# Four unused tensors in the SBUF layout of a transformer layer's kernel

## The reference

```python
u = x * (1.0 + sc1) + sh1
x = layer_norm(ALPHA * x + 0.5 * (1.0 + g1) * swiglu(u, ffn1_wg[l], ffn1_wu[l], ffn1_wd[l]), ln_g[l, 0], ln_b[l, 0])
u = x * (1.0 + sc2) + sh2
h = u @ w_in[l]
...
y = jnp.concatenate([o_nsa, o_mla], axis=-1) @ w_out[l]
x = layer_norm(ALPHA * x + (1.0 + g2) * y, ln_g[l, 1], ln_b[l, 1])
u = x * (1.0 + sc3) + sh3
x = layer_norm(ALPHA * x + 0.5 * (1.0 + g3) * swiglu(u, ffn2_wg[l], ffn2_wu[l], ffn2_wd[l]), ln_g[l, 2], ln_b[l, 2])
```

## The kernel before

| stage | stationary | moving | before | with the change |
|---|---|---|---|---|
| `ffn1A` | left, `ffn1A_*_hi/lo` | right, `ffn1S_*` | 160 and 0 | 0 and 0 |
| `ffn1B` | left, `ffn1B_h_*` | left, `ffn1B_wd_*` | 160 and 160 | 0 and 0 |
| `in` | right, `mix_in_u_*` | left, `in_w_*` | 0 and 128 | 0 and 0 |
| sparse, scores | left, `nsa_q` | left, `sparse_k_*` | 192 and 128 | 0 and 0 |
| sparse, apply | left, `sparse_v` | left, `nsaa_turned_*` | 128 and 192 | 0 and 0 |
| latent inputs | left, `queries_q_*`, `latent_kv_*` | left, `latent_in_uq_*`, `latent_ukv_*` | 128 and 128 | 0 and 0 |
| latent, scores and apply | left, `mla_q_*`, `latent_v` | left, `mla_k_*`, `mlaa_turned_*` | 128 and 128 | 0 and 0 |
| `out` | right, `mix_out_u_*` | left, `out_w_*` | 0 and 128 | 0 and 0 |
| `ffn2A` | left, `ffn2A_*_hi/lo` | right, `ffn2S_*` | 0 and 0 | 0 and 0 |
| `ffn2B` | left, `ffn2B_h_*` | left, `ffn2B_wd_*` | 0 and 0 | 0 and 0 |

## Time and profile before

### The profile page before, as it was taken

The page is one execution under the profiler, slowest core; times in us unless marked ns, Lnnn a source line. Parts: engine busy times, 40 slices in busy tenths (PEclk is TensorE's granted clock), DMA queues, the critical chain, the costliest instruction groups (busy, mean ns, idle before and its releaser), DMA issues. The chain is left out here.

```text
span 2456.2 us, 29088 instructions
## 1 busy us (share of the span) xinstructions
PE 2212.3 (90%) x10593; PEld 1824.4 (74%) x10593; DVE 1514.7 (62%) x2164; ACT 963.8 (39%) x1874; POOL 815.6 (33%) x665
## 2 busy tenths in 40 slices
PE   3899999979998899799998899896899999969993
PEld 3677888868887688688887788784688888857783
DVE  6866777636556614487887577635754445457667
ACT  4222323322234221777876466515333333312222
POOL 4355556534442000132211000003344444334443
PEclk9899999989998899899998899898899999989997
DMA  6244554344442310300000000312122222254442
GB/s 243 82 146 155 168 170 155 120 163 142 153 138 74 127 47 29 110 1 1 1 1 1 1 1 1 114 33 103 60 78 78 88 93 77 86 193 133 142 144 109
DMA packets 167875, 230.84 MB, mean 94 GB/s; under 512 B 15473, under 2 KB 113841, under 8 KB 167736
## 3 DMA queue, kind: packets, MB, share of 16 engines
q1 hardware_dynamic: 159672, 199.65, 24.8%
q0 software_dynamic: 8064, 29.36, 3.5%
HBM read 193.32 MB, written 35.66 MB: 93 GB/s over the span
## 5 line engine op out<-in xcount | busy, mean ns | idle before, releaser
L623 POOL TENSOR_TENSOR ffn_raw_u<-ffn_raw_u,ffn_gate 128x1024 f32<-128x1024 f32 x44 | 115.5, 2625 | 150.4 <-DMA ffn_raw_u<-in_ffn_wd 150.2
L663 PE MATMUL ffn_banks<-ffn2B_wd_hi,ffn2B_h_hi 128*128 128x512 f32 x352 | 140.1, 398 | 21.1 <-DVE ffn2B_h_lo L643 20.9
L623 POOL TENSOR_TENSOR ffn_raw_g<-ffn_raw_g,ffn_gate 128x1024 f32<-128x1024 f32 x44 | 109.6, 2490 | 138.3 <-DMA ffn_raw_g<-in_ffn_wd 132.4
L663 PE MATMUL ffn_banks<-ffn1B_wd_hi,ffn1B_h_hi 128*128 128x512 f32 x352 | 138.2, 393 | 13.4 <-DVE ffn1B_h_lo L643 13.4
L663 PE MATMUL ffn_banks<-ffn2B_wd_hi,ffn2B_h_lo 128*128 128x512 f32 x352 | 137.9, 392 | 0.0
L663 PE MATMUL ffn_banks<-ffn2B_wd_lo,ffn2B_h_hi 128*128 128x512 f32 x352 | 137.9, 392 | 0.0
L663 PE MATMUL ffn_banks<-ffn1B_wd_lo,ffn1B_h_hi 128*128 128x512 f32 x352 | 137.5, 391 | 0.0
L663 PE MATMUL ffn_banks<-ffn1B_wd_hi,ffn1B_h_lo 128*128 128x512 f32 x352 | 137.5, 391 | 0.0
L575 DVE TENSOR_TENSOR ffn2A_u<-ffn2A_u,ffn_banks 128x512 f32<-128x512 f32 x66 | 45.4, 687 | 144.5 <-PE ffn_banks L544 136.4
L544 PE MATMUL ffn_banks<-ffn1S_s_hi,ffn1A_t_hi 128*128 128x512 f32 x264 | 106.4, 403 | 12.8 <-DVE ffn1S_s_lo L490 12.8
L544 PE MATMUL ffn_banks<-ffn2S_s_hi,ffn2A_t_hi 128*128 128x512 f32 x264 | 103.8, 393 | 12.8 <-DVE ffn2S_s_lo L490 12.8
(11 more groups left out here) (383 smaller groups left out, 6699.4 us busy)
## 6 DMA issues: line engine op xcount, KB each, us to landing
ada_rows<-in_w_ada POOLq DMA_DIRECT2D x56, 512.0 KB, 4.7
ffn_raw_g<-in_ffn_wg SPq DMA_DIRECT2D x44, 512.0 KB, 3.9
ffn_raw_u<-in_ffn_wu SPq DMA_DIRECT2D x44, 512.0 KB, 5.2
ffn_raw_g<-in_ffn_wd SPq DMA_DIRECT2D x44, 512.0 KB, 3.5
ffn_h_raw<-hidden SPq DMA_DIRECT2D x88, 256.0 KB, 3.6
ffn_raw_u<-in_ffn_wd SPq DMA_DIRECT2D x44, 512.0 KB, 3.6
early_w<-in_w_ada SPq DMA_DIRECT2D x16, 512.0 KB, 7.6
early_x<-in_x SPq DMA_DIRECT2D x4, 2048.0 KB, 13.7
```

Of the source, the lines that this page charges most:

```text
L623: pool.tensor_tensor(self.wd(n), self.wd(n), self.gate[:, :], ALU.mult).then_inc(self.gated, 1)
L663: last = pe.matmul(self.banks[:, at, :], h[m][:, i * P:(i + 1) * P], w[m][:, e * HALF:(e + 1) * HALF], start=(f == 0 and p == 0), stop=(f ...
```

## The change

Four tensors are allocated and never used: 128 bytes per partition ahead of `all_ident` at the very start of the left side, 224 bytes in the first FFN behind `ffn1_c_col`, 192 bytes behind `sparse_rstd` ahead of the sparse stages, and 128 bytes in the second FFN behind its `ffn2_offset`. Everything allocated after one of them on the left, within its scope, moves up by its size. No instruction is added, taken away or moved. The right side stays where it is.

```diff
@@ feed_forward_first @@
     norm_rows, c_col = s.sb("norm_rows", [8 * DC, P]), s.sb("c_col", [P, DC])
+    s.sb("base", [P, 56])
     ffn = SplitFfn(nc, s, "ffn1", *weights, h_dram, ident)
@@ feed_forward_last @@
     gain, offset = s.sb("gain", [P, DC]), s.sb("offset", [P, DC])
+    s.sb("base", [P, 32])
     ffn = SplitFfn(nc, s, "ffn2", *weights, h_dram, ident)
@@ layer @@
     with Scope(nc, "all") as a, Scope(nc, "far", side="right") as far:
+        a.sb("base", [P, 32])
         ident = a.sb("ident", [P, P])
@@ layer @@
                 rstd = b.sb("rstd", [P, 2, TT])
+                b.sb("base", [P, 48])
                 sparse_inputs(nc, "sparse_in", h, table, gates, ident, (cmp_k_pos, cmp_v_pos), (cmp_k_w1, cmp_v_w1),
```

## The result

| | before | with the change |
|---|---|---|
| median | 2457.24 us (6 runs, 2454.80 to 2461.55) | 2443.58 us (6 runs, 2442.26 to 2447.62) |
| ratio of times, changed to before, and its 95% interval | | 0.9946 (0.9934 to 0.9959) |
| span of the profiled execution | 2456.2 us | 2440.5 us |
| mean granted clock | 0.956 | 0.955 |

The change makes the kernel 13.7 us faster by the medians; the two profiled executions differ by 15.7 us.

What follows compares the result with a forecast made beforehand. The prediction took the kernel to be bound by how often PE can start a matmul in stretches without waits. Savings of 7.9 + 1.5 + 5.6 + 2.2 + 0.5 = 17.7 us took 2457.9 to 2440 us, range 2433 to 2451 (8 in 10).

Steps and rivals of the forecast that it cites:

- The reading of the cause: Gapless matmul streams: 13.4 ns above the columns when both operands' remainders modulo 256 agree, 19 to 20 ns otherwise.
- Step 1: First FFN's product phase, ffn1A: spacing falls from 233.4 to 226.7 ns; 7.9 us steady plus 1.5 us early.
- The steady part: Last 14 of ffn1A's 22 steps, 1176 matmuls saving 6.7 ns each: 7.9 us.
- The early part: First 8 steps of ffn1A, where PE waits for DVE: 1.5 us taken, 4.5 at most, below nothing possible.
- Step 2: Input projection `in`, 768 matmuls of 494 columns saving 7.3 ns each: 5.6 us, bounds 0 and 5.6.
- Rival A: Odd width: `in` keeps 226.5 ns because 494 columns fall out of step with weight loads; 2446, chance 0.13.
- Step 3: Output projection `out`, 384 matmuls saving 5.6 ns each, from 232.3 to 226.7: 2.2 us.
- Step 4: Sparse attention, operands brought to equal remainders: 2 ns for 440 wide matmuls, 0.9 us at most, 0.5 taken.
- Step 5: ffn1B, ffn2A, ffn2B and the latent inputs keep equal remainders: 0 us.
- rival B: Gain given back in the down projection: ffn1B falls into ffn2B's slower rhythm, 8.0 us; 2448, chance 0.11.
- Rival C: Remainders aren't the cause; something else slows ffn1A and the projections, and stays; 2458, chance 0.08.
- Rivals D and E: First: operands at equal places modulo 2048 collide, 2463, chance 0.05. Second: pads misplace an operand; no sum changes, no chance given.

Runs made afterwards that it cites:

- k1_both_160: Changed kernel with both operands of ffn1A at 160, only the stationary one of ffn2A at 160, weights of both projections at 64; 2457.27 us.
- k3_128_64_192: Changed kernel with the stationary operand at 128 in ffn1A and 64 in ffn2A, the moving one at 192 in `in` and `out`; 2464.93 us.
- k4_small_shifts: Changed kernel with the stationary operand at 224 in ffn1A and 32 in ffn2A, the moving one at 32 in `in`, 160 in `out`; 2469.62 us.
- k7_changed_again: The changed kernel measured a second time, nothing altered; median 2441.13 us, ratio to before 0.9927.
- k2_moving_160: Changed kernel with ffn2A's moving operand at 160, ffn1A's stationary at 192, both operands of `in` at 128, `out`'s weights at 32; 2464.65 us.
- k12_whose_weights: Changed kernel with only u_lo of `out` at 128 and the four weight buffers of `in` at 96, 112, 128 and 160; 2444.17 us.
- k11: Changed kernel with the four weight buffers of `in` at 176, 184, 192 and 224; 2440.84 us.
- k6: Changed kernel with both projections put back to their layout before the change, weights at 128; median 2443.72 us, ratio to before 0.9943.
- k10: Changed kernel with the weights of `in` at 192; median 2437.72 us, ratio to before 0.9928.

## Why the prediction was right, and where it wasn't

The forecast was 2440 with a range of 2433 to 2451; the median is 2443.6. The sum was 17.7 us, of which 13.7 came by the medians and 15.7 by the two profiled executions. The stages that the sum names gave 13.5 us (9.4 + 2.4 + 1.6 + 0.1); that the profiled total is nearer to the forecast is luck, by the 2.1 us between stages, which the sum doesn't have.

*The reading of the cause* (equal remainders) holds for all streams of 512 columns. The decisive evidence ahead of the change was `ffn1B`, fast at 160 and 160; `k1_both_160` made the same in `ffn1A`, and made `ffn2A` slow by 160 and 0.

*Step 1, `ffn1A`.* The steady part is exact: a step of 84 matmuls went from 19.60 to 19.04 us, 14 of them 7.8 us (forecast 7.9), and neither DVE nor POOL became the limit. The early part was forecast at 1.5 and came at 1.6, but that agreement is luck. The early windows shown above have PE busy 58.9 of 60 us and 73.4 of 80, the latter at a mean clock of 0.96 where it was 1.00 before. Part of this is a stretch of 3.4 us at the lower level, in these windows of before and of the changed kernel:

```profile
169.00:177.00 8.00, 5.34 (x23) 4.37 (x24) 7.50 (x8) 4.18 (x8) 6.82 (x7) 1.00 0.25 69
169.00:177.00 8.00, 5.89 (x20) 4.56 (x19) 7.23 (x8) 4.44 (x8) 6.83 (x7) 0.79 0.27 84
```

It is there, near 170 us, in all eleven traces with `ffn1A` at 226.7 or 228.9 ns and in none of the three at 233.3; what brings it isn't shown. At half the clock it can take back up to 1.7 us of PE's time. The prediction named a falling clock as a risk and gave it no price of its own. PE's and DVE's waits there in the changed kernel, to set beside the earlier trace rows (waited for: us in total, times, longest us):

```profile
PE ffn_banks L544 <- DVE ffn1A_u L575: 7.6, 5, 3.3
```

```profile
DVE ffn1A_c L575 <- DMA hidden<-ffn1A_c: 25.2, 6, 5.3
DVE late_part_late L864 <- DMA ada_rows<-in_w_ada: 13.0, 7, 3.2
...
DVE ffn1A_c L575 <- PE ffn_banks L544: 3.0, 3, 1.6
```

The last of them was, before:

```profile
DVE ffn1A_c L575 <- PE ffn_banks L544: 9.5, 4, 3.7
```

As argued, the faster PE arrives sooner at the same chain: DVE's wait for the stores of the hidden tile grew from 18.4 to 25.2 us, its wait for PE fell from 9.5 to 3.0, and their sum stayed at 28 us; PE's own wait for L575 went from 8.6 to 7.6, so the sign that the prediction named for a failure of this step, a growing wait, didn't come. How much of the 4.5 us gets through differs from one execution to the next. Over the nine traces with `ffn1A` at 0 and 0 the stage took 456.6 to 462.0 us, with the changed kernel's 462.0 the longest and a middle value of 459.1. Against the one trace of before (471.4) that is 9.4 to 14.8. So the early part gave between 1.6 and 7.0, beyond the upper bound of 4.5, which priced only the matmuls' own spacing. But before's 471.4 looks like a long one: the two other traces with `ffn1A` at 233.3 ns, `k3_128_64_192` and `k4_small_shifts`, have 468.9 and 469.1. Against their 469.0 the early part gave -0.8 to 4.6, about what the prediction allowed.

*Step 2, `in`.* This is the term that was mis-sized: 5.6 us forecast, 2.4 measured (1.4 in `k7_changed_again`, where PE also waited 8.1 us for the first weights in place of 7.2). The spacing fell to 223.4, not to 219.2, so the sign that the prediction set for itself, 219 to 220 ns, failed. The step took the excess of the 512- and 384-column streams, 13.4 ns, over to 494 columns; at equal remainders it is 17.5 for 494 (and 16.6 for 480). Rival A was half right: the width does put `in` out of step, but the start matters all the same, only with its best place elsewhere (192). No row of before had a 494-column stream at another remainder, and the range said so; the value taken lay at the far end of 0 to 5.6 where the middle, 2.8, would have been close.

*Step 3, `out`.* Spacing 232.3 to 227.0, as forecast. The stage lost 1.6 of the 2.2 us here and 2.5 in `k7_changed_again`.

*Step 4, attention.* 0.1 us of 0.5. A sooner PE may gain nothing there at its waits for ACT and DVE, as in step 1's early part; no run separates this. The price of 2 ns was that of the apply matmul, whose difference was 64; the scores had 192, which costs 6.6 ns in `ffn2A` of `k3_128_64_192`, so 0.9 us was too low as an upper bound, and what the stage held back is more than the 0.4 us between forecast and result.

*Step 5 and rival B.* `ffn2A` and `ffn2B` are unchanged within 0.5 us. The prediction put the 0.1 us between a load's landing in `ffn1B` and in `ffn2B` down to the remainder; in the changed kernel, with both at 0, `ffn_raw_g` still lands in 3.6 and 3.5 us, so the 0.1 belongs to the stage, and no run shows a load that lands sooner. `ffn1B` wasn't thrown into the slower rhythm of `ffn2B`: 256.1 us. But rhythms of this kind exist. Over the traces here `ffn1B` at equal remainders took 255.3 to 260.6 us, the longest in `k2_moving_160`; so something like rival B is worth up to 5 us, and little of it fell on the change (0.8 us). What makes it isn't shown: PE's waits for L643 and its like in that stage add up to under 1 us more in `k2_moving_160` than before.

*Rival C* is out by `k1_both_160`. The Trainium skill says on it ("TensorE: Matmul & The Clock Gate", Part 2, step-by-step) that the array has two independent read ports and that the load of the next weights takes no read bandwidth from the running matmul. The runs don't agree with what the prediction drew from this, that the places of the operands can't matter: with the same instructions, the distance went from 226.7 to 234.3 ns by where they lie, and in `k12_whose_weights` to 232.3 where only the weights being loaded lay elsewhere. Whether it is read bandwidth that is lost, no run shows.

*Rivals D and E* are out: `ffn1A` is at 226.6 and `ffn2A` at 226.7 ns with both operands at 0 modulo 2048, and the shifts did what the layout table said.

## What to carry to other kernels

When a matmul stream of this kind has no gaps and its distance from start to start is more than that of a neighbour stage with the same shape, compare the start of the two SBUF operands modulo 256 bytes before looking at anything else; pads of 32 to 224 bytes changed it by up to 3% here, and the wrong pads cost 12 us in all. Make them equal for 512 or 384 columns, and for an odd width try a few starts, since no rule found here gave the best one. What such a gain is worth is only what the stretch without waits holds: count its matmuls, and give those ahead of a wait a range.

## What the runs showed of the hardware

Distance from start to start of float32r matmuls, 128 x 128 stationary, at 2.4 GHz, by the moving operand's remainder minus the stationary one's (modulo 256). A mean over the later part of a stage, where PE had no gap, from the stages and runs named; those of `k11` and `k12` for 494 columns are from one weight buffer in four.

| difference | 512 columns, ns | where | 494 columns, ns | where |
|---|---|---|---|---|
| 0 | 226.7 | `ffn2A` before; changed; `ffn1A` `k1` | 223.4 | changed; `k2` |
| 32 | 233.3 | `out` `k2`; `ffn1A` `k4` | 223.3 | `k4` |
| 64 | 228.9 | `out` `k1`; `ffn1A` `k2` | 225.3 | `k1` |
| 96 | 233.3 | `ffn1A` before; `ffn2A` `k1` | 224.5 | `k12` |
| 128 | 232.4, 233.3 | `out` before; `ffn1A` `k3` | 226.7 | before; `k6` |
| 160 | 234.3 | `out` `k4`; `ffn2A` `k2` | 220.3 | `k12` |
| 192 | 233.3 | `out`, `ffn2A` `k3` | 220.0 | `k3`, `k10` |
| 224 | 233.3 | `ffn2A` `k4` | 226.6 | `k11` |

Between 384 and 512 columns at a difference of 0 lie 226.7 - 173.3 = 53.4 ns for 128 columns, one cycle of 2.4 GHz each. Above their 213.3 ns, 512 columns pay 13.3 ns at a difference of 0, which is 32 cycles, and 20 ns, 48 cycles, at most others. 384 columns pay 13.3 at 0 and 64 and 16.7 at 96; 480 columns pay 16.6 at 0 and 17.7 or 20.1 at 128. That the price depends on the difference and not on the stage is shown (seven of the eight differences have two stages or kernels at 512 columns, within 0.1 ns but for 128, where `out` and `ffn1A` are 0.9 apart). That 256 bytes is a period is shown too: the `ffn2A` tensors lay at 1792 modulo 2048 before and at 0 after, with the moving operand at 0, and ran at 226.7 ns both times, while no smaller shift that was tried left 512 columns at that. Why the period is 256 bytes, why 64 is cheaper, and why 494 columns are best at 192 or 160 isn't shown; no rule that was tried (equal remainders, the end of the row on 256, the length of the row) gives all values of the table. The fastest stream that any layout might allow to 494 columns is therefore unknown; with the 13.3 ns of 512 columns it would be 219.2, and 220.0 was reached.
